# One decoder layer on one core: a projection half unit behind the turn of k, a shorter norm chain, an earlier start of the output product, the shared weight scaled before the output loop, and tile 5 of the shared expert split

## What is computed

```python
h = _rms(x) * norm1_g * (1 + sc1) + sh1
proj = h @ w_in                      # 16 blocks of 512 columns, and the gate rows
y_fox = forgetting attention         # 8 heads
y_ml  = mLSTM, chunkwise             # 4 heads
oh    = _hgrn2_chunkwise(q, k, v, logf)          # 4 heads of 128
y_hg  = _rms(oh) * hgrn_norm_g * silu(hg)
merged = sum(sigmoid(gate_b) * (y_b @ w_branch[b]))   # b = 0, 1, 2
x = x + g1 * (merged @ w_out)
h = _rms(x) * norm2_g * (1 + sc2) + sh2
shared = (silu(h @ ws1) * (h @ ws3)) @ ws2
x = x + g2 * (experts(h) + shared)
```

## Time and profile before

| what | value |
|---|---|
| time, median of 3 runs | 2608.07 us (2606.92 to 2609.73) |
| the profiled execution's own time | 2606.76 us |
| its span in the profile | 2605.0 us |
| PE busy | 2515.9 us (97%) |
| DVE, ACT, POOL busy | 1045.5, 586.3, 421.0 us (40%, 23%, 16%) |
| granted TensorE clock, mean | 0.996 |

### The profile page before, as it was taken

The page is one execution under the profiler, slowest core; times in us unless marked ns, Lnnn a source line. Parts: engine busy times, 40 slices in busy tenths (PEclk is TensorE's granted clock), DMA queues, the critical chain, the costliest instruction groups (busy, mean ns, idle before and its releaser), DMA issues.

```text
span 2605.0 us, 30862 instructions
## 1 busy us (share of the span) xinstructions
PE 2515.9 (97%) x9358; PEld 1273.0 (49%) x9359; DVE 1045.5 (40%) x2664; ACT 586.3 (23%) x1080; POOL 421.0 (16%) x421
## 2 busy tenths in 40 slices
PE   6999999999999999999999999999999999999996
PEld 3444555555455556555444454444444444444443
DVE  3376443443565645554244756121122122222221
ACT  3311332333312332331111121111111111111121
POOL 0000000000201000000110434222222222222222
PEclk9999999999999999999999999999999999999999
DMA  8222232433623232223333116876889789989874
GB/s 263 59 45 82 75 115 89 122 96 84 200 47 81 72 97 89 76 82 110 109 109 125 57 41 251 298 260 213 279 274 363 265 276 356 350 269 345 306 247 107
DMA packets 128415, 441.80 MB, mean 170 GB/s; under 512 B 18268, under 2 KB 20452, under 8 KB 111168
## 3 DMA queue, kind: packets, MB, share of 16 engines
q1 hardware_dynamic: 86560, 306.91, 33.4%
q0 software_dynamic: 41760, 133.64, 19.2%
HBM read 370.63 MB, written 77.20 MB: 172 GB/s over the span
## 4 chain that ended last, share of the span: by engine, by line
PE 86%; DMA 8%; issue 2%; DVE 2%; ACT 1%; POOLq 0%; POOL 0%; DVEq 0%; SPq 0%; ACTq 0%
PE psum L858 34%; PE psum L1253 13%; PE psum L1274 7%; DMA out_x<-work,put 7%; PE psum L1116 6%; PE psum L1131 4%; PE psum L1257 2%; PE psum L1073 2%; PE psum L1247 2%; PE psum L1175 2%; PE psum L952 2%; PE psum L942 2%; PE psum L961 1%; PE psum L1281 1%; DMA work<-h_d,idx 1%
## 5 line engine op out<-in xcount | busy, mean ns | idle before, releaser
L858 PE MATMUL psum<-hT,ring 128*128 128x512 f32 x1152 | 511.1, 593 | 0.0
L858 PE MATMUL psum<-ring,hT 128*128 128x512 f32 x896 | 398.4, 596 | 2.0 <-ACT hT L1461 2.0
L858 PEld LDWEIGHTS psum<-hT,ring 128*128 128x128 f32 x1152 | 211.6, 190 | 231.0 <-issue 230.6
L858 PEld LDWEIGHTS psum<-ring,hT 128*128 128x128 f32 x896 | 166.0, 191 | 187.9 <-issue 187.2
L1253 PE MATMUL psum<-hT,work 128*128 128x512 f32 x560 | 247.6, 595 | 8.4 <-issue 3.9
L2337 DVE TENSOR_TENSOR work<-work,psum 128x256 f32<-128x256 f32 x93 | 39.2, 421 | 444.8 <-ACT work L1711 434.4
L1253 PE MATMUL psum<-ring,work 128*128 128x512 f32 x448 | 197.7, 594 | 3.1 <-issue 1.7
L1508 ACT ACTIVATE work<-psum 128x512 f32<-128x512 f32 x128 | 76.2, 596 | 508.2 <-PE psum L858 505.3
L712 POOL DMA_INDIRECT work<-h_d,idx x96 | 98.6, 1027 | 550.7 <-issue 262.2
L716 POOL DMA_INDIRECT out_x<-work,put x93 | 142.7, 1534 | 192.9 <-issue 162.3
L1253 PEld LDWEIGHTS psum<-hT,work 128*128 128x128 f32 x560 | 103.9, 190 | 130.6 <-issue 130.6
(11 more groups left out here) (392 smaller groups left out, 2793.8 us busy)
## 6 DMA issues: line engine op xcount, KB each, us to landing
ring<-in_exp_w SPq DMA_DIRECT2D x100, 1024.0 KB, 12.0
hT<-in_exp_w SPq DMA_DIRECT2D x68, 1024.0 KB, 9.2
work<-in_exp_w SPq DMA_DIRECT2D x33, 1024.0 KB, 13.6
ring<-in_w_in SPq DMA_DIRECT2D x16, 2048.0 KB, 13.5
proj_d<-work SPq DMA_DIRECT2D x104, 256.0 KB, 2.0
work<-in_ada_w POOLq DMA_DIRECT2D x16, 1024.0 KB, 5.8
work<-proj_d POOLq DMA_DIRECT2D x56, 256.0 KB, 2.9
work<-proj_d POOLq DMA_DIRECT2D x20, 512.0 KB, 5.0
```

Of the source, the lines that this page charges most:

```text
L858: mm = t.matmul(bank(unit_bank(u)), l, r, start=(k == 0), stop=(k == KD - 1))
```

## The change

1. `HG_FILL`: the half unit of place 11 (one of four) goes to place 9, between the turn of k and the state update.
2. `rms_scale`: the first guess takes one instruction in place of two, a Newton step three in place of four; 11 in place of 15.
3. The multiplication by `ghg` is applied to silu(hg) ahead of the wait for `h_up`, no longer to the normalised output after it.
4. PE starts the output product when 31 of 32 merges are there; tile 4, the first that reads tokens 512 to 1023, waits for the last.
5. The scaling of `shw2` moves from `residual(3)` to the place ahead of `residual(0)`, with its two waits.
6. `shared_up(5)` is cut: three of its eight products go between the turn and the router product of tile 7.

```diff
-        HG_FILL = [8, 1, 1, 1, 1, 1, 1, 1, 0, 0, 1, 4]
+        HG_FILL = [8, 1, 1, 1, 1, 1, 1, 1, 0, 1, 1, 3]
...
-            link(v.tensor_scalar(y.bitcast(I32), x.bitcast(I32), 1, None, ALU.logical_shift_right))
-            link(v.tensor_scalar(y.bitcast(I32), y.bitcast(I32), -1.0, float(0x5F3759DF), ALU.mult, ALU.add))
+            link(v.tensor_scalar(y.bitcast(I32), x.bitcast(I32), -0.5, float(0x5F3759DF), ALU.mult, ALU.add))
             for step in range(3):
                 link(v.tensor_tensor(z, y, y, ALU.mult))
-                link(v.tensor_tensor(z, z, x, ALU.mult))
-                link(v.tensor_scalar(z, z, -0.5, 1.5, ALU.mult, ALU.add))
-                link(v.tensor_tensor(out_ if step == 2 else y, y, z, ALU.mult))
+                link(v.scalar_tensor_tensor(out=z, in0=z, scalar=-0.5, in1=x, op0=ALU.mult, op1=ALU.mult))
+                link(v.scalar_tensor_tensor(out=out_ if step == 2 else y, in0=z, scalar=1.5, in1=y, op0=ALU.add, op1=ALU.mult))
...
-            pe.wait_ge(s_mg, 32)
+            pe.wait_ge(s_mg, 31)
...
+                if i == NT // 2 and half == 0:
+                    pe.wait_ge(s_mg, 32)
...
             route_turn(7)
+            shared_up(5, 0, 3)
             route(7)
             rank(6)
-            shared_up(5)
+            shared_up(5, 3, KD)
...
                 take(7)
+                link(v.tensor_tensor(c8(hg), c8(hg), ghg[:, h * P:(h + 1) * P].unsqueeze(1).to_broadcast([P, NT, P]), ALU.mult))
...
-                link(v.tensor_tensor(c8(hE0), c8(hE0), ghg[:, h * P:(h + 1) * P].unsqueeze(1).to_broadcast([P, NT, P]), ALU.mult))
...
             dve.wait_ge(s_ls, 16)
+            dve.wait_ge(s_w2, 16 * FK)
+            dve.wait_ge(s_gm, 32)
+            for k in range(FK):
+                ins = v.tensor_tensor(shw2[k], shw2[k], g2b, ALU.mult)
+            ins.then_inc(s_wo, 1)
...
-                if i == 3:
-                    dve.wait_ge(s_w2, 16 * FK)
-                    dve.wait_ge(s_gm, 32)
-                    for k in range(FK):
-                        ins = v.tensor_tensor(shw2[k], shw2[k], g2b, ALU.mult)
-                    ins.then_inc(s_wo, 1)
```

More of the change, by code:

```diff
@@ L1163, in _, with shared_up @@
             up_bank = lambda i: (0, 1, 2)[i - 5] if i >= 5 else 2
-            def shared_up(i):
-                if i == 0:
+            def shared_up(i, first=0, end=KD):
+                if first > 0:
+                    pass
+                elif i == 0:
                     block_ready(pe, ("sh", 0))
@@ L1173, in shared_up @@
                     pe.wait_ge(s_x2, NT)
-                for k in range(KD):
+                for k in range(first, end):
                     mm = t.matmul(bank(up_bank(i)), h2T[:, k, i * P:(i + 1) * P], slot(("sh", 0))[:, k, :], start=(k == 0), stop=(k == KD - 1))
-                mm.then_inc(s_H, 1)
+                if end == KD:
+                    mm.then_inc(s_H, 1)
             def shared_turn(i):
```

## The result

The changed kernel took **2613.96 us** (median of 13 runs, 2612.9 to 2618.6) against 2609.49 us of the kernel before (13 runs, the three of its table among them; no chip is on record for this group): ratio 1.0019, 95% interval 1.0011 to 1.0026. The forecast was 2602.5, with a range up to 2606.0. It was wrong, and in the direction to which I gave 0.04. The profiled execution took 2613.44 us for a span of 2611.7.

A forecast was written before the change was run, and what follows sets the result against it. The prediction took PE's own time line as the bound (86% of the chain that ended last); -5.56 + 2.70 - 2.35 - 0.4 = -5.6 us off the median gave 2602.5 us, with a range of 2599.5 to 2606.0.

The forecast's parts named there:

- Half unit, -5.56: HGRN state update: a half unit ahead of it removes PE's wait for ACT's copy of k, 1.39 us in each of four heads.
- Early start of the output product, swallowed: Output product: its 1.74 us wait goes, but PE stops later at tile 0's turn, so nothing is gained.
- Early scaling, +2.70: Ahead of residual(0): DVE waits for ws2 until 1400.3, then scales, so PE goes on at tile 0's turn 2.70 us later.
- a wait of 5.5 us there: Ahead of tile 0's turn: PE's wait grows from 1.05 to some 5.5 us, released by DVE.
- Tile 3, -2.35: From residual(3) to the shared expert's hidden tile: DVE's chain is 2.35 us shorter, leaving 0.19 of PE's 2.54 us wait.
- Tile 5 split, -0.4: Tile 7's router product: six records fill PE's wait; DVE's later queue leaves a gain of 0.4 us, bounds 0 and 1.3.
- a wait of 0.75 at `shared_turn(5)` where 0.9 was forecast: At `shared_turn(5)`: PE would arrive at 1584.85 and wait 0.9 us for DVE, whose queue ends at 1585.75.
- Sum: Whole kernel: -5.56 + 2.70 - 2.35 - 0.4 = -5.6 us, giving 2602.5 us.
- the "slower" rival: ws2's transfer lands 10.8 us later, at 1411, holding residual and PE: 2613.3 us, 0.2% slower; chance 0.04.
- the forecast had 1.5 either way: Expert stage: taken over as a shift, with nine PE waits that may come out otherwise, 1.5 us either way.

The follow-up runs named there:

- e13: The changed kernel unaltered, run again on chip 9: 2604.16 us, ratio 0.9984 to the kernel before.
- e15: The kernel before, unaltered, as a run of its own on chip 9: 2606.56 us, ratio 0.9998.
- e10: The changed kernel with the scaling of ws2 back in residual(3), split of tile 5 kept, on chip 3: 2600.18 us, ratio 0.9970.
- e9: The kernel before, unaltered, as a run of its own on chip 3: 2609.93 us, ratio 1.0004.
- e6: The changed kernel with 24 small DVE instructions between the scaling of ws2 and residual(0), chip 12: 2616.95 us, ratio 1.0025.
- e7: The changed kernel with two products of shared_up(5) ahead of tile 7's router product in place of three, chip 12: 2613.80 us, ratio 1.0012.
- e11: The changed kernel unaltered, run again on chip 3: 2605.42 us, ratio 0.9991.
- e18: The kernel before, unaltered, as a run of its own on chip 7: 2607.16 us, ratio 0.9999.
- e1: The changed kernel with shared_up(5) whole again behind the ranking (no split), chip 0: 2605.03 us, ratio 0.9988.
- e2: The changed kernel with the scaling of ws2 back in residual(3), split of tile 5 kept, chip 0: 2600.42 us, ratio 0.9970.
- e4: The kernel before with the split of tile 5 alone, chip 0: 2605.76 us, ratio 0.9994.
- e12: The changed kernel without the split of tile 5 and with the scaling of ws2 behind residual(0), chip 3: 2598.99 us, ratio 0.9964.
- e17: The changed kernel with the scaling of ws2 behind residual(0), split of tile 5 kept, chip 7: 2604.57 us, ratio 0.9986.
- groups B and E: Follow-up runs on chips 12 and 7: the changed kernel, variants of it and, on chip 7, the kernel before; 2604.42 to 2616.95 us and 2604.57 to 2612.53 us.
- e3: The changed kernel with both the split of tile 5 and the early scaling of ws2 undone, chip 0: 2601.75 us, ratio 0.9971.

## Why the prediction was wrong, step by step

The sum was -5.6 us, and the result lies 4.5 us on the other side. The clean comparison is e13 with e15, one chip, no late signals. PE's lead of the changed kernel there: 5.46 us at the first branch product, 1.61 at tile 0's turn, 2.24 at tile 7's, 3.05 at L1234 and at the first expert row.

1. **Half unit, -5.56.** Right: 5.46 here, 5.52 over the four heads of the first profile. No wait ahead of the turn of y, and the norm chain, the gain and the next head cost nothing.
2. **Early start of the output product, swallowed.** Right for this kernel. With the scaling in residual(3) it is kept: in e10 tile 0's and tile 7's turns lead those of e15 by 1.84 and 1.85 us more than the branch products do, against 1.74 for the wait that went (e9, on e10's own chip, gives 1.84 at tile 0, and at tile 7 has 1.7 us of half clock of its own).
3. **Early scaling, +2.70.** The mechanism was right, the size was not: 3.85 (5.46 - 1.61). The distance from `residual(0)` to the turn is 7.69, as the forecast had it (7.72), and the first load takes the 13.4 of the earlier trace rows; but the second takes 9.8 to 10.4 us in the 15 profiles with the early output product, against 8.9 to 9.3 in the five without it. On chip 9 it is 10.3 (e13) against 9.2 (e15), 1.1 of the 1.15 us that 2.70 lacked. I took the landing as fixed to its issue.
4. **A term that was missing: the clock.** In the wait of 6.8 us PE's granted clock falls to half, 1.2 GHz, for 6.8 us, of which 3.4 lie behind the wait (1404.0 to 1410.8 in the first profile, and the wait ends at 1407.4): +1.67 us (from tile 0's turn to tile 7's e13 gains 0.63 where 2.3 was due). I forecast a wait of 5.5 us there and priced it at its length. The Trainium skill ("TensorE: Matmul & The Clock Gate", HAM oscillation) says that a wait for DMA can throttle PE again, so that what follows starts cold; the traces agree (PE waits for DVE here, and DVE for the transfer). In e6 the wait is 10.0 us and the half clock lasts from 1402.5 to 1416.1; in e7 and e11, with waits of 6.8 and 7.0, it lasts 10.2 us.
5. **Tile 3, -2.35.** Right: the wait went from 2.54 to 0.28. Together with 3 and 4 the early scaling costs 5.1 us against e10 (tile 7's turn less branch products: +3.22 against -1.85), where +2.1 was forecast (2.70 - 2.35 and the 1.74 given up). e10 is 5.2 us faster than e11 on the same chip.
6. **Tile 5 split, -0.4.** It gives 0.81, and a wait of 0.75 at `shared_turn(5)` where 0.9 was forecast.
7. **Sum.** Without late signals -3.05 in the profile up to the experts, -3.5 and -3.9 in the medians: 2604 to 2605.5, in the range. In the one pair of profiles the experts then took 2.8 us more in e13 than in e15, so the whole executions differ by 0.2; the medians are the better measure of the sum. The forecast of 2602.5 was too low by 1.15 (step 3) and 1.67 (step 4), less 0.4 (step 6).
8. **The step that failed** is the end of the one on tile 5, "Left: -0.4 us", with nothing behind it: the sum has no term for the stretch from `shared_turn(5)` to the experts. I followed the tail only to there and took it that a signal of PE arrives when its product ends. In the first result it did not: +7.28 us from L1234 to L1237 and +2.45 from there to the experts, where the clock is half (the stages in the section on the result). These 9.7 us are nearly all of the 9.8 between 2614.0 and the 2604.2 of e13. No rival named this; the "slower" rival was the landing of ws2, which slipped by 1.2 us and not by 10.8.

**What stays open.** Shown is: late signals and missing records belong to some chips (or to something that came with them) and not to the change: the kernel before has both on chip 7 (e18), the changed kernel neither on chips 3 and 9. PE waits for them in every such trace of a kernel with both the split and the scaling ahead of tile 1 (six on chips 12 and 7, and the first profile), and not in e18. Not run on such a chip: e1, e2, e4, e12. So whether the split is what exposes the kernel is not settled. One difference would fit: with the split `slots(7)` is ready earlier, and POOL issues the 16 list stores of tiles 6 and 7 without the pause of 1.2 us between the two eights that the kernel before has; the first late signal of this stretch is that of `shared_up(6)` in the first profile, and in e18 that of `shared_down(5)`, two signals further on. That was not tried by itself. Every execution here was recorded, and where the signals are late a part of the records is missing. The Trainium skill ("NOTIFIC — the notification-queue block", Overflow: three behaviours, one of which stalls the engine) says that the block that writes such records, when its ring is full, drops new ones, overwrites old ones or stalls the producer, as it is set. If something of this kind is at work, the wait is one of the recording and absent from an unrecorded execution. No run here shows whether it is, and what the first profile shows is not a stalled PE but late signals of a PE that goes on.

**The best version** on record is e12, 2598.99 us (ratio 0.9964), on a chip without late signals: the half unit, the norm chain, the early output product, the scaling behind residual(0), no split. Its trace has 1.7 us of half clock in tile 7 (1565.0 to 1568.4), 2.6 us behind the wait of 1.1 us ahead of the router product that the split takes away. With the split (e17), on a chip with late signals, the same scaling took 2604.57 where the changed kernel took 2612.53; on a chip without them this version was not run.

## What to carry to other kernels

Put a wait for a transfer where the waiting engine idles behind its urgent work, not in front of it: two multiplications moved past one function cost 5 us in the one place and nothing in the other. Price a wait of PE with the half clock that can follow it: after waits of 5.6 to 10.0 us here it came each time, after 2.5 us in half of the traces. And before an unexplained difference is put down to an edit, run both kernels on the same chip with a trace of each, and look for late signals where nobody waits for them too: three runs here (e1 to e3) seemed to take a wait away that their chip never had.

## What the runs showed of the hardware

- In eight traces (the first of the changed kernel, those of groups B and E) there are 7 to 8% fewer semaphore records (15.2 to 15.4 thousand against 16.5 to 16.6). In these, PE's signals came 4 to 8 us late in one stretch (2.2 and 2.5 us in the kernel before), while POOL issued 16 small indirect stores, and a few came up to 1.7 us late elsewhere. In the twelve other traces no recorded signal of PE is later than 0.6 us.
- A short wait of PE can be followed by half clock, worth 1.7 us for a stretch of 3.4. Eight traces have the wait of 2.5 us ahead of the shared expert's first turn, and four of them (e2, e3, e4, e9) have such a stretch at its end; of the twelve in which the early scaling took the wait away none has. Two (e9, e12) of the eight with 1.1 us ahead of tile 7's router product have one 2.6 us behind it. So these edits can give more than the wait itself. At 205 us six of the 20 traces have one without a wait, behind 2.1 us of 4x4 transposes. Timeline of e9, where 8 transposes take 1.70 us from start to start, and the window's row with the granted clock:

```profile
1468.03 0.69 PE L1183 MATMUL psum<-ident,work 128*128 128x128 f32 x2 [2.53 <-DVE work L2235]
1468.52 1.92 PE L1142 MATMUL psum<-ident,work 128*128 128x128 f32 x8
```

```profile
1467.60:1471.00 3.40, 2.97 (x11) 2.53 (x12) 0.38 (x1) 0.92 (x2) 0.55 (x1) 0.51 0.01 0
```

- The expert stage, whose instructions were the same in all kernels, differed by -1.9 to +2.5 us from the first profile's; the forecast had 1.5 either way.
